# A two-layer diffusion trunk on one core: softmax divided after the values product, other banks in attention, two modulation chunks on TensorE

## The reference

```python
def modulation(cond, w_mod, b_mod):
    m = jax.nn.silu(cond) @ w_mod + b_mod        # 1024 -> 6 * 1024, for two conditions
    return jnp.split(m[:, None, :], N_MOD, axis=-1)

    def one_block(qi):                           # 128 queries, 8 heads, 2 key/value heads
        s = jnp.einsum('bqkgd,bskd->bkgqs', qi.astype(jnp.float32), kf) * scale
        p = jax.nn.softmax(s, axis=-1)
        return jnp.einsum('bkgqs,bskd->bqkgd', p, vf).astype(q.dtype)

def trunk_layer(x, cond, ctx_k, ctx_v, p):
    sh1, sc1, gt1, sh2, sc2, gt2 = modulation(cond, p['w_mod'], p['b_mod'])
    h = rms_norm(x, p['norm1_g']) * (1.0 + sc1) + sh1
    q, k, v, u = mixer_projections(h, p['w_in'], p['q_norm_g'], p['k_norm_g'])
    ...
    mix = jnp.concatenate([attn, pooled.astype(attn.dtype)], axis=-1) @ p['w_out']
    x = x + gt1 * mix
    h2 = rms_norm(x, p['norm2_g']) * (1.0 + sc2) + sh2
    x = x + gt2 * conv_ffn(h2, p['w_up'], p['conv_w'], p['conv_b'], p['w_down'])
```

## Time and profile before

| | us |
|---|---|
| median of 3 runs | 1502.22 (1500.97 to 1504.16) |
| profiled execution: its time | 1499.22 |
| profiled execution: its span | 1497.4 |
| TensorE busy | 1427.3 (95%) |
| VectorE busy | 942.9 (63%) |
| ScalarE busy | 517.0 (35%) |
| input projection of layer 0 / layer 1 | 95.8 / 86.8 |
| attention of layer 0 / layer 1 | 96.4 / 85.1 |
| output projection of layer 0 / layer 1 | 58.1 / 56.4 |

### The profile page before, as it was taken

One profiled execution on the slowest core, in us unless ns is written; L12 is line 12 of the kernel. 1 busy time (PEld: TensorE's weight loads), 2 busy tenths in 40 slices (PEclk: granted clock), 3 DMA queues, 4 the chain that ended last, 5 costly groups with the idle time before them and its releaser, 6 DMA issues.

```text
span 1497.4 us, 25179 instructions
## 1 busy us (share of the span) xinstructions
PE 1427.3 (95%) x10013; PEld 1382.7 (92%) x10013; DVE 942.9 (63%) x1410; ACT 517.0 (35%) x742; POOL 398.1 (27%) x259
## 2 busy tenths in 40 slices
PE   7987889999999999999999979999999999999996
PEld 4987679999999999999999967999999999999996
DVE  3997995799784658794854778339944323444323
ACT  3335672343222123323132567324322212332321
POOL 0274001124441014343214500122433101323320
PEclk9999899999999999999999989999999999999998
DMA  9541112425434424344512200132422321222321
GB/s 337 181 129 31 57 58 74 153 79 160 126 116 141 152 89 149 114 126 125 157 54 71 75 1 1 34 108 73 132 78 79 94 67 58 83 70 71 97 59 70
DMA packets 191870, 147.05 MB, mean 98 GB/s; under 512 B 4384, under 2 KB 179112, under 8 KB 190760
## 3 DMA queue, kind: packets, MB, share of 16 engines
q1 hardware_dynamic: 190592, 145.32, 31.5%
q10 hardware_dynamic: 1192, 0.52, 0.1%
HBM read 142.94 MB, written 2.88 MB: 97 GB/s over the span
## 4 chain that ended last, share of the span: by engine, by line
PE 82%; DVE 9%; issue 3%; ACT 2%; POOL 1%; DMA 1%; SPq 0%; DVEq 0%; ACTq 0%; POOLq 0%
PE pair L1169 69%; PE pair L1186 4%; DVE mod_acc L845 3%; PE pair L1451 2%; PE pair L1429 2%; PE pair L1416 2%; DVE small L1054 1%; PE pair L1256 1%; DVE w_lo L822 1%; POOL tree L486 1%; PE pair L1287 1%; DMA xin<-in_x_sample_dram 1%; ACT tree L732 1%; PE pair L1239 0%; DVE conv L1113 0%
## 5 line engine op out<-in xcount | busy, mean ns | idle before, releaser
L1169 PE MATMUL pair<-in_hi,w_hi 128*128 128x320 f32 x1792 | 411.6, 311 | 10.0 <-DVE w_lo L822 10.0
L1169 PE MATMUL pair<-in_hi,w_lo 128*128 128x320 f32 x1792 | 409.1, 310 | 0.0
L1169 PE MATMUL pair<-in_lo,w_hi 128*128 128x320 f32 x1792 | 409.0, 310 | 0.0
L1169 PEld LDWEIGHTS pair<-in_hi,w_hi 128*128 128x128 f32 x1792 | 299.9, 188 | 11.9 <-issue 8.8
L1169 PEld LDWEIGHTS pair<-in_lo,w_hi 128*128 128x128 f32 x1792 | 300.3, 188 | 0.0
L1169 PEld LDWEIGHTS pair<-in_hi,w_lo 128*128 128x128 f32 x1792 | 300.1, 188 | 0.0
L1113 DVE SCALAR_TENSOR_TENSOR conv<-pair,vec,conv 128x127 f32<-128x127 f32 x352 | 168.7, 541 | 200.4 <-ACT conv L760 200.3
L517 POOL TENSOR_TENSOR silu_a<-silu_a,conv 128x640 f32<-128x640 f32 x44 | 110.8, 2519 | 561.2 <-DVE conv L1113 561.2
L822 DVE TENSOR_TENSOR w_lo<-w_raw,w_hi 128x1024 fp32r<-128x1024 f32 (+1 forms) x152 | 203.4, 1339 | 41.7 <-ACT w_hi L538 41.5
L538 ACT ACTIVATE w_hi<-w_raw 128x1024 fp32r<-128x1024 f32 (+1 forms) x88 | 103.2, 1173 | 353.8 <-PE pair L1169 323.7
L845 DVE SCALAR_TENSOR_TENSOR mod_acc<-mod_raw,cond,mod_acc 128x1024 f32<-128x1024 f32 x140 | 221.6, 1624 | 0.0
(11 more groups left out here) (164 smaller groups left out, 1547.7 us busy)
## 6 DMA issues: line engine op xcount, KB each, us to landing
w_raw<-in_w_up_dram SPq DMA_DIRECT2D x88, 512.0 KB, 3.9
mod_raw<-in_w_mod_dram SPq DMA_DIRECT2D x80, 512.0 KB, 3.9
w_raw<-in_w_down_dram SPq DMA_DIRECT2D x32, 704.0 KB, 4.6
w_raw<-in_w_in_dram SPq DMA_DIRECT2D x20, 512.0 KB, 4.0
w_first<-in_w_mod_dram SPq DMA_DIRECT2D x8, 1024.0 KB, 14.6
w_raw<-in_w_out_dram SPq DMA_DIRECT2D x16, 512.0 KB, 4.2
out_dram<-yout SPq DMA_DIRECT2D x5, 512.0 KB, 3.9
xin<-in_x_sample_dram SPq DMA_DIRECT2D x4, 512.0 KB, 6.6
```

The costliest lines, as they stand in the source:

```text
L1169: ins = pe.matmul(dst[:, a:a + HALF_T], w[:, s, k, :], rhs[:, kk, a:a + HALF_T], start=first and r == 0, stop=last and r == 2)
```

## The change

1. The probabilities are no longer divided before they are transposed. `transpose_prob` waits for the exponentials alone. The row sums go to `den`; once a block DVE takes 8 reciprocals (`rden`), PE spreads them over the partitions (`spread_sums`, 4 small matmuls a half block, 64 columns of weights each), DVE copies the result (`o_factor`), and `o_norm` multiplies the block's outputs by it. `o_low` and ACT's copy then read `o_normed` in SBUF.
2. Transposed tiles go to `turned[i % 2]`, two banks in turn, and the last tile (layer 0) or the last two (layer 1) to the bank `shared`; ACT copies the first 4 (3) tiles, DVE the others (`last_tiles`). Outputs of all blocks go to one bank, `o_bank`.
3. `weigh_pair` is cut in two: key tiles 0 to 2 in the even step, 3 and 4 in the odd one.
4. Chunks 2 and 3 of layer 0 are computed together by `mod_second`, as `mod_first` does it: 8 calls of 4 matmuls in the input projection of layer 0, from 8 loads of 1 MB, then one copy, 4 transposes and two short `mod_finish`. The passes, reductions and `mod_reduce` of these chunks are gone. The key statistic goes to `lin[2]` instead of `lin[3]`.

```diff
@@ places @@
-        cond_cols = mod_acc[:, 0, 0:NK * QUAD].rearrange("p (k r) -> p k r", k=NK)
+        cond_cols = ssum[:, 0:NK * QUAD].rearrange("p (k r) -> p k r", k=NK)
+        second_place = [t[:, :, :].rearrange("p s d -> p (s d)") for t in (mod_raw, mod_acc)]
+        second_rows = mod_acc[:, 0, 0:512]
+            den, rden = (k_rstd[:, i * NU:(i + 1) * NU] for i in range(2))
+            o_normed, o_factor = (rope[:, i, :].rearrange("p (t c) -> p t c", t=NQ) for i in range(2))
+        turned = [pair[2][:, 0:512], pair[3][:, 512:1024]]
+        shared = pair[2][:, 512:1024]
+        o_bank = pair[3][:, 0:NQ * P].rearrange("p (t c) -> p t c", t=NQ)
+        def by_scalar(L, i):
+            return 1 if UNITS[i][0] == 0 else NT - (1 if L == 0 else 2)
+        def factor_half(i):
+            return (i // NH - 1, i % NH) if i >= NH and i % NH < 2 else None
@@ SyncE: one load of 1 MB per k holds chunks 2 and 3 @@
+            def load_second(k):
+                if k == 0:
+                    sp.wait_ge(s_xsq, NT)
+                elif k == 1:
+                    sp.wait_ge(s_ft, 1)
+                else:
+                    sp.wait_ge(s_second, k - 1)
+                sp.dma_start(second_place[k % 2], w_mod[0, k * P:(k + 1) * P, 2 * D:4 * D]).then_inc(s_sld[k % 2], 16)
...
-                    for k in units_at.get(n, ()):
-                        load_mod(2, k, k % 2)
-                    if L == 0 and n in (4, 5):
-                        load_mod(3, n - 4, n - 4)
+                    if L == 0 and 1 <= n < NK - 1:
+                        load_second(n + 1)
                 if L == 0:
-                    for k in range(2, NK):
-                        load_mod(3, k, k % 2)
+                    sp.wait_ge(s_second, NK)
@@ ScalarE @@
+                    if L == 0 and n == NK:
+                        act_e.wait_ge(s_second, NK)
+                        act_e.activation(second_rows, pair[3][:, 512:1024], ACT.Copy).then_inc(s_srow, 1)
...
-                                         accum_out=small[:, i % 3, 1:2]).then_inc(s_exp, 1)
+                                         accum_out=den[:, i:i + 1]).then_inc(s_exp, 1)
...
-                        nkeys = P if UNITS[j][0] == 0 else T
+                        nkeys = P * by_scalar(L, j)
-                        act_e.activation(prob_place[j % 4][:, 0:nkeys], pair[2][:, 0:nkeys], ACT.Copy).then_inc(s_pte, 1)
+                        act_e.activation(prob_place[j % 4][:, 0:nkeys], turned[j % 2][:, 0:nkeys], ACT.Copy).then_inc(s_pte, 1)
@@ VectorE @@
+            def o_norm(L, pos):
+                dve.wait_ge(s_o, L * NU + (pos + 1) * NH)
+                dve.wait_ge(s_of, 2 * (L * NT + pos + 1))
+                dve.tensor_tensor(o_normed, o_bank, o_factor, ALU.mult).then_inc(s_on, 1)
+            def last_tiles(L, j):
+                ns = by_scalar(L, j)
+                dve.wait_ge(s_pt, L * NU + j + 1)
+                if UNITS[j][0] != 0:
+                    if j >= 4:
+                        dve.wait_ge(s_o, L * NU + j - 3)
+                    dve.tensor_copy(prob_place[j % 4][:, ns * P:T], shared[:, 0:T - ns * P]).then_inc(s_ptv, 1)
+                if factor_half(j) is not None:
+                    pos, half = factor_half(j)
+                    if L * NT + pos > 0:
+                        dve.wait_ge(s_on, L * NT + pos)
+                    dve.tensor_copy(o_factor[:, 2 * half:2 * half + 2, :],
+                                    shared[:, 256:512].rearrange("p (t c) -> p t c", t=2)).then_inc(s_of, 1)
...
-                    for k in units_at.get(n, ()):
-                        mod_unit(2, k, k % 2)
-                    if L == 0 and n == 5:
-                        mod_part_sums(2)
+                    if L == 0 and n == N_IN - 1:
+                        mod_finish(2)
+                        mod_finish(3)
...
-                    if i > 0:
-                        un, j = L * NU + i - 1, (i - 1) % 3
-                        nkeys = P if UNITS[i - 1][0] == 0 else T
-                        dve.wait_ge(s_exp, un + 1)
-                        dve.reciprocal(small[:, j, 2:3], small[:, j, 1:2]).then_inc(s_rec, 1)
-                        dve.wait_ge(s_rec, un + 1)
-                        dve.tensor_scalar(prob[j][:, 0:nkeys], prob[j][:, 0:nkeys],
-                                          small[:, j, 2:3], None, ALU.mult).then_inc(s_prob, 1)
+                    if i >= NH + 4 and (i - 4) % NH == 0:
+                        o_norm(L, (i - 4) // NH - 1)
+                    if i >= 2:
+                        last_tiles(L, i - 2)
+                    if i > 0 and i % NH == 0:
+                        pos = i // NH - 1
+                        dve.wait_ge(s_exp, L * NU + i)
+                        dve.reciprocal(rden[:, pos * NH:i], den[:, pos * NH:i]).then_inc(s_rec, 1)
-                    if 5 <= i and (i - 4) % NH == 0:
-                        o_low(L, (i - 4) // NH - 1)
-                    if L == 0 and i % 2 == 0 and 4 <= i < 4 + 4 * NK:
-                        k = i // 4 - 1
-                        mod_unit(3, k, k % 2, (i % 4 // 2,))
-                    if L == 0 and i == 4 + 4 * NK:
-                        mod_part_sums(3)
+                    if i >= NH + 6 and (i - 6) % NH == 0:
+                        o_low(L, (i - 6) // NH - 1)
@@ TensorE @@
+            def mod_second(k):
+                pe.wait_ge(s_sld[k % 2], 16 * (k // 2 + 1))
+                for j in range(4):
+                    ins = pe.matmul(pair[3][j * QUAD:(j + 1) * QUAD, 512:1024], cond_cols[:, k, :],
+                                    second_place[k % 2][:, j * 512:(j + 1) * 512], start=k == 0, stop=k == NK - 1)
+                ins.then_inc(s_second, 1)
...
                     linear(tile_in(L) + n, n % 2, NK, in_hi, in_lo)
...
+                    if L == 0 and n < NK:
+                        mod_second(n - 1)
+                        if n == NK - 1:
+                            mod_second(n)
...
                 def transpose_prob(i):
-                    pe.wait_ge(s_prob, un + 1)
-                    if i > 0:
-                        pe.wait_ge(s_pte, un)
+                    pe.wait_ge(s_exp, un + 1)
+                    if i > 1:
+                        pe.wait_ge(s_pte, un - 1)
...
+                    for kt in range(ns):
+                        ins = pe.transpose(turned[i % 2][:, kt * P:(kt + 1) * P], prob[i % 3][:, kt * P:(kt + 1) * P], ident)
+                    if i > 0 and (UNITS[i][0] != 0 or factor_half(i) is not None):
+                        pe.wait_ge(s_ptv, moved(L, i - 1))
...
+                    if factor_half(i) is not None:
+                        pos, half = factor_half(i)
+                        ins = spread_sums(L, pos, half, shared[:, 256:512])
+                    if UNITS[i][0] != 0:
+                        for kt in range(ns, NT):
+                            ins = pe.transpose(shared[:, (kt - ns) * P:(kt - ns + 1) * P],
+                                               prob[i % 3][:, kt * P:(kt + 1) * P], ident)
+                def spread_sums(L, pos, half, dst):
+                    pe.wait_ge(s_rec, L * NT + pos + 1)
+                    for t in range(2):
+                        for side in range(2):
+                            u_ = pos * NH + 2 * (2 * half + t) + side
+                            ins = pe.matmul(dst[side * HALF:(side + 1) * HALF, t * P:(t + 1) * P],
+                                            rden[:, u_:u_ + 1].to_broadcast([P, HALF]), ident, start=True, stop=True)
-                def weigh_pair(i):
+                def weigh_pair(i, part):
...
-                    for kt in range(nkt):
+                    for kt in range(min(nkt, 3)) if part == 0 else range(3, nkt):
...
-                for i in range(NU + 3):
-                    if i >= 4 and i % 2 == 0:
-                        weigh_pair(i - 4)
+                for i in range(NU + 4):
+                    if i >= 4:
+                        weigh_pair(i - 4 - i % 2, i % 2)
```

More of the change, by code:

```diff
@@ L280, in mlp_chunks, with moved, factors_done @@
             return [C if C < DEPTH * N_MOD else None for C in range(first, first + 3)]
-        def o_bank(pos):
-            return pair[3][:, (pos % 2) * 512:(pos % 2) * 512 + NQ * P].rearrange("p (t c) -> p t c", t=NQ)
+        def by_scalar(L, i):
+            return 1 if UNITS[i][0] == 0 else NT - (1 if L == 0 else 2)
+        def moved(L, i):
+            return L * (NU - NH) + sum(UNITS[j][0] != 0 for j in range(i + 1))
+        def factor_half(i):
+            return (i // NH - 1, i % NH) if i >= NH and i % NH < 2 else None
+        def factors_done(L, i):
+            return 2 * L * NT + sum(factor_half(j) is not None for j in range(i))
         def rq_of(sign, i):
@@ L348, in _ @@
             sp.dma_start(cst[:, P:n_const], consts[:, P:n_const]).then_inc(s_const, 16)
-            sp.wait_ge(s_xsq, NT)
-            for s in range(2):
-                load_mod(2, s, s)
+            load_second(0)
```

(21 more changed lines are left out.)

75 lines of the change are left out of this document (43 added, 32 removed).

## The result

| | us |
|---|---|
| before, median of 20 runs | 1502.99 (1498.32 to 1507.27) |
| after, median of 20 runs | 1506.23 (1504.52 to 1511.06) |
| ratio after to before | 1.0022, 95% interval 1.0014 to 1.0030 |
| profiled execution of after | 1506.08, span 1504.3 |

The change made the kernel slower by 3.2 us. I had forecast 1500.8, a gain of 1.4.

The account below looks back on a forecast made before the run. TensorE, busy 95% of the span, was taken as the bound. Layer 1's attention +4.5, layer 0's -6.8, input projection +1.6 and output projection -0.7 summed to -1.4 us: 1500.8 from 1502.22, range 1497 to 1505.

Parts of the forecast that it names:

- The step that failed: VectorE in layer 1's attention: loop through its new copy, 3.93 against TensorE's 4.18, covered; 1.0 us, bounds 0 and 5.
- covers: Layer 1's attention: added work fits into TensorE's waits for exponentials and the tail; -2.6 us, bounds 0 and 3.
- my terms without VectorE: Layer 1's attention: -7.2 transposes' places, +6.6 cut product, +6.7 factors, -2.6 covers.
- my sum: Layer 1's two latent blocks: eight pairs at 4.18 instead of 4.20, four half blocks of factors, 0.5 for VectorE; +3.7.
- the loop through the last tiles' copy becomes the bound: Slower rival, attention: with a loop of 4.4, each of 32 latent pairs takes 0.2 more; 1507.2 us, chance 0.15.
- The three slower rivals: VectorE's copy loop as bound, 0.15; last `mod_second` waiting for its load, 0.10; transposes still waiting, now for `s_ptv`, 0.05.
- VectorE's 0.2 to 0.4 in hand: Attention's latent pairs: margin of VectorE's loop, 3.93, under TensorE's list, 4.18; given as evidence against the loop rival.
- the bank waits: Layer 1's attention: transposes' wait of 0.43 a pair for ACT's copy goes; gain 7.2 us, bounds 5.4 and 8.
- the factors: `spread_sums` on TensorE's list, ten half blocks a layer with added array switches; +6.7 us, bounds 4.2 and 10.9.
- The rival in which the last `mod_second` waits 3 us for its load: Slower rival, layer 0's input projection: the wait and a clock fall behind it, +5.0, 1505.8 us; chance 0.10.
- the cut: Values product in two: one more entry and exit of the halved array, 0.41 a latent pair; +6.6 us a layer.
- the drain: Skill's figure near 175 ns per tiling switch: two are 0.35 instead of 0.41, kernel's sum 2.6 us lower; not taken.

Follow-up runs that it names:

- e6_bare: The changed kernel with the values product whole and without the factors, outputs copied undivided (softmax's division left out): 1492.54 us, ratio 0.9939 to before.
- e3_modonly: The kernel before with the modulation part alone (chunks 2 and 3 on TensorE), attention as before: 1489.16 us, ratio 0.9909 to before.
- e1_uncut: The changed kernel with the values product whole again in the even step, all else as changed: 1508.78 us, ratio 1.0041 to before.
- e9_later: The changed kernel with VectorE's copies of last tiles and factors one unit later, same instructions: 1492.40 us, ratio 0.9938 to before.
- e7_actlast: The changed kernel with the values product whole, last tiles and factors copied by ScalarE instead of VectorE: 1493.00 us, ratio 0.9936 to before.

## Why the prediction was wrong

**The step that failed** is the one on VectorE, with the "covers" behind it: "This copy waits for transposes and stands ahead of the next maximum", a loop of 3.93 against a list of 4.18, "covered"; 1.0 us a layer, bounds 0 and 5. By the reordering it cost 93.81 - 87.65 = 6.2 in layer 1 and 93.88 - 86.44 = 7.4 in layer 0, outside both bounds. I had the loop, its members and nearly its length (3.93, and 3.85 in e6_bare). I then compared it with TensorE's list in one place only, the steady pair, and there it is covered indeed. A layer has three other places. In the first four units TensorE has no product yet, and a pair of its list is 2.3, so the loop sets the pace: 4.0 us more (18.97 against 14.99 with the other order), of which 1.5 is TensorE's clock behind the wait of 2.18. For that the prediction had no term in attention; it let the clock fall in one rival only. At the way back from prompt to latent units: 1.8 (13.46 against 11.70). In each latent block the block's own work on VectorE (`o_norm`, `o_low`, reciprocals, factor copies), which I take to lengthen the loop there: 18.72 against 17.70, 1.0, where I had put 0.25. That the order costs this is shown; which of the block's operations does it was not tried apart. The periods of the four pairs (maxima of every second unit from 22) read 4.05, 4.46, 5.86, 4.35 in the change and 4.06, 4.06, 4.79, 4.80 with the other order. Back the other way goes 0.5 in the prompt block. Sum for layer 1: 4.0 + 1.8 + 2.0 - 0.5 = 7.3; the stretches ahead of the first maximum (0.9) and behind unit 38's (0.3) return 1.2.

**The covers** had the wrong sign for the same reason. I took 2.6 off since TensorE waits at the start anyhow, so that work added to it costs nothing. That holds for work on TensorE. But where TensorE waits another chain is the bound, and this change lengthened that chain too. With the other order the covers are there: layer 1's attention is 2.6 longer than before, where my terms without VectorE give +3.5.

**Luck.** For the two latent blocks my sum has +3.7 and +3.9 was measured, but its terms are off and cancel. A steady pair takes 4.06 instead of 4.18 (-1.0 for eight) and a half block of factors 0.73 instead of 0.83 (-0.4), while VectorE took 2.0 instead of 0.5 (+1.5).

**The rival** "the loop through the last tiles' copy becomes the bound" gave 1507.2 for the measured 1506.2, and I gave it 0.15. Its place was wrong (all 32 pairs by 0.2; it was the first block, the way back to latent units and one pair of each block), its mechanism right, and so its number is near by luck. The three slower rivals had 0.30 between them, where the prediction's last line on chances gives "slower" 0.25. What I said speaks against it, "VectorE's 0.2 to 0.4 in hand", is a number of the steady pair.

**Right:** the bank waits are gone (no transposes in the list of waits); the factors cost 6.45 for 6.7 in layer 1 (8.3 in layer 0); `mod_second` 1.00 to the next instruction; layer 0's attention without modulation as layer 1's (84.57 and 85.07 in e3_modonly), so that part gained what it should: 13. For the input projection I had +1.6 over before; it is +0.4 here and +1.3 in e3_modonly. The rival in which the last `mod_second` waits 3 us for its load did not come: no such wait is above 0.3. In the output projection the wait for the low parts stayed at 1.26 although `mod_finish` had left VectorE's list: -0.2 for -0.7. Why was not tried.

**Half right:** the cut. I read one more entry and exit as 0.41, from products of different length; side by side it is 0.35 (4.05 against 3.70). So the steady pair is 4.06 for 4.18: 0.06 less for the switches, and 0.07 less since the pair without the wait is 3.70 and not 3.77. The 0.35 is also the estimate that the prediction worked out from the drain, and set aside. But in the change, and with the order mended, taking the cut away gains next to nothing in a block of layer 1 (18.81 for 18.72; 17.47 for 17.70). In these two, waits for exponentials and for `o_norm` fill what the whole product frees. That an even spread of TensorE's work over the two steps of a pair is worth as much as the switches cost is what I argue from this, and no run here shows it apart. The Trainium skill (page "TensorEngine Tiling (Array Packing)", section Key Properties) says that a change of tiling mode drains TensorE. The 0.35 agrees with that; the near equal times of the other two show that its price need not be on the path.

## What to carry to other kernels

When an engine gets an operation that waits for a later stage, ask what stands behind it in its list and whether that is ready already; compare the resulting loop with the bound at every kind of place (start, change of block, tail), not only in the steady state. Stretches where the bounding engine waits are cover for work on that engine alone; for the engine that it waits for they are the critical path. If such a loop is found, try first to let the copy stand one unit later: here that was worth 13 us with not one instruction changed.

## What the runs showed of the hardware

Outside attention the kernels after, e1_uncut, e9_later and others have the same instructions, and yet the time between the two attentions differs: 628.5 us in after, 631.2 in e1_uncut. The granted clock of TensorE differs there. After, then e1_uncut:

```profile
730.00:772.00 42.00, 41.40 (x294) 41.07 (x292) 26.16 (x32) 10.20 (x13) 7.28 (x7) 1.00 0.35 101
```

```profile
730.00:772.00 42.00, 41.42 (x284) 41.28 (x283) 24.59 (x31) 9.47 (x11) 6.52 (x6) 0.96 0.35 101
```

0.04 of 42 us is 1.7 us, and e1_uncut has 284 matmuls in this stretch where after has 294. The lower level stands near the start and the end of an MLP, where TensorE waits a little: from 290 to 296 us the granted clock is 0.72 in after and 0.51 in e1_uncut. So an edit in attention can go with up to 4 us elsewhere (628.1 in e9_later, 632.2 in e7_actlast). In e1_uncut it is 2.7 between the attentions and 1.3 behind the second, which outweighs the 1.9 that its attentions are shorter. Executions of one kernel differ in the same way: e7_actlast took 1489.1 at a granted clock of 0.992 and 1495.5 at 0.986. So a difference of 2 or 3 us between two medians here says little by itself; what is said of the cut rests on the blocks inside attention. What decides where the clock falls was not tried.
